# First mixer's head sums in column tiles, and factors spread through device memory

## What is computed

```python
def _rms_norm(x, w):
    xf = x.astype(jnp.float32)
    y = xf * lax.rsqrt(jnp.mean(xf * xf, axis=-1, keepdims=True) + EPS)
    return (y * w.astype(jnp.float32)).astype(x.dtype)
def _rms_f32(xf):
    return xf * lax.rsqrt(jnp.mean(xf * xf, axis=-1, keepdims=True) + EPS)
def _l2norm(xf):
    return xf * lax.rsqrt(jnp.sum(xf * xf, axis=-1, keepdims=True) + EPS)
...
    q = _l2norm(q.reshape(bsz, s, h, d)) * (d ** -0.5)
    k = _l2norm(k.reshape(bsz, s, h, d))
...
    o = _rms_f32(_from_chunks(o))
```

## Time and profile before

| | |
|---|---|
| median of 3 runs | 1778.69 us (1778.51 to 1781.49) |
| profiled execution | 1779.13 us |
| its span, first to last instruction | 1777.3 us |
| mean granted TensorE clock | 0.998 |
| PE busy | 1752.7 us, 99% |
| DVE busy | 1152.7 us, 65% |
| ACT busy | 722.4 us, 41% |
| DMA queue of SP | 172.01 MB, 30.0% of 16 engines |

### The profile page before, as it was taken

One profiled execution on the slowest core, in us unless ns is written; L12 is line 12 of the kernel. 1 busy time (PEld: TensorE's weight loads), 2 busy tenths in 40 slices (PEclk: granted clock), 3 DMA queues, 4 the chain that ended last, 5 costly groups with the idle time before them and its releaser, 6 DMA issues.

```text
span 1777.3 us, 22802 instructions
## 1 busy us (share of the span) xinstructions
PE 1752.7 (99%) x9216; PEld 1393.8 (78%) x9216; DVE 1152.7 (65%) x1685; ACT 722.4 (41%) x1026; POOL 0.2 (0%) x4
## 2 busy tenths in 40 slices
PE   8999989999999999999999999999998999999999
PEld 6777867888888887776888888888764888888887
DVE  5876944777776344777777777433997667777521
ACT  4257424544444333445644444323224544444321
POOL 0000000000000000000000000000000000000000
PEclk9999999999999999999999999999999999999999
DMA  6222111322332322311332222232652222332222
GB/s 232 95 95 72 43 33 42 134 95 95 98 102 79 110 97 94 107 44 52 123 103 95 95 95 94 96 98 96 191 173 82 96 95 95 98 102 95 88 97 79
DMA packets 57969, 173.60 MB, mean 98 GB/s; under 512 B 8316, under 2 KB 9084, under 8 KB 57736
## 3 DMA queue, kind: packets, MB, share of 16 engines
q1 hardware_dynamic: 57720, 172.01, 30.0%
q10 hardware_dynamic: 144, 0.13, 0.0%
HBM read 161.32 MB, written 2.12 MB: 92 GB/s over the span
## 4 chain that ended last, share of the span: by engine, by line
PE 96%; DVE 2%; ACT 1%; issue 1%; DMA 0%; SPq 0%; DVEq 0%; ACTq 0%
PE bank L201 95%; DVE mixer_arena L1216 1%; PE bank L645 0%; DMA res<-in_x 0%; DVE mixer_arena L1224 0%; DVE res L1216 0%; DVE even_arena L1752 0%; ACT even_arena L777 0%; DVE mixer_arena L1515 0%; ACT wh L777 0%; DVE mixer_arena L1220 0%; DVE wl L1216 0%; DVE gdn_low_ygl L1216 0%; PE bank L413 0%; ACT conf_rstd L777 0%
## 5 line engine op out<-in xcount | busy, mean ns | idle before, releaser
L201 PE MATMUL bank<-nh,wh 128*128 128x512 f32 x1504 | 596.0, 396 | 0.0
L777 ACT ACTIVATE wh<-raw 128x1024 fp32r<-128x1024 f32 (+2 forms) x308 | 306.8, 998 | 697.3 <-PE bank L201 688.6
L201 PE MATMUL bank<-nh,wl 128*128 128x512 f32 x1504 | 586.6, 390 | 0.9 <-issue 0.9
L201 PE MATMUL bank<-nl,wh 128*128 128x512 f32 x1504 | 586.2, 390 | 0.0
L1216 DVE TENSOR_TENSOR wl<-raw,wh 128x1024 fp32r<-128x1024 f32 (+2 forms) x308 | 352.8, 1146 | 242.1 <-ACT wh L777 241.3
L201 PEld LDWEIGHTS bank<-nh,wh 128*128 128x128 f32 x1504 | 282.7, 188 | 69.5 <-issue 11.4
L201 PEld LDWEIGHTS bank<-nl,wh 128*128 128x128 f32 x1504 | 282.9, 188 | 61.7 <-issue 3.4
L201 PEld LDWEIGHTS bank<-nh,wl 128*128 128x128 f32 x1504 | 282.7, 188 | 60.5 <-issue 1.4
L201 PE MATMUL bank<-ff_yh,wh 128*128 128x512 f32 x528 | 205.4, 389 | 0.0
L201 PE MATMUL bank<-ff_yl,wh 128*128 128x512 f32 x528 | 205.4, 389 | 0.0
L201 PE MATMUL bank<-ff_yh,wl 128*128 128x512 f32 x528 | 205.4, 389 | 0.0
(11 more groups left out here) (188 smaller groups left out, 1420.6 us busy)
## 6 DMA issues: line engine op xcount, KB each, us to landing
raw<-in_ff_a_up SPq DMA_DIRECT2D x44, 512.0 KB, 3.4
raw<-in_ff_b_up SPq DMA_DIRECT2D x44, 512.0 KB, 3.4
raw<-in_ff_c_up SPq DMA_DIRECT2D x44, 512.0 KB, 3.4
raw<-in_w_in SPq DMA_DIRECT2D x32, 512.0 KB, 3.6
raw<-in_pw SPq DMA_DIRECT2D x24, 512.0 KB, 3.7
raw<-in_even_in SPq DMA_DIRECT2D x16, 512.0 KB, 3.5
conf_shifted<-conf_pad SPq DMA_DIRECT2D x112, 66.0 KB, 2.0
raw<-in_ff_a_down_a SPq DMA_DIRECT2D x8, 512.0 KB, 3.5
```

What stands on the lines that cost most here:

```text
L201: return e.matmul(out, lhsT, rhs, start=start, stop=stop, skip_group_check=True)
L777: return e.activation(out, in_, func, **kw).then_inc(n.give(sem), 1)
```

## The change

Head sums: the twelve sums of full width become three groups of four. In a group g each sum has 32 columns of ones as its stationary operand and writes 32 rows of one bank, so that the four heads' sums stand in rows 0, 32, 64 and 96 of that bank. One logarithm and one exponential then serve four heads. As the factor is no longer on every partition, SP stores the four rows to device memory (store_heads) and reads them back as one row of 2048 values into all 128 partitions (spread_heads), over the four squares' slots; DVE waits for that transfer (head_spread) before the first of each four scales. ACT takes the first root before it squares the queries. The squares of the retention outputs move to other slots.

Value factor: root_columns and ACT's copy are gone. SP stores row 0 of c.r and issues four transfers of 128 values, one value to a partition, at pieces 9 and 11 of the first mixer and at pieces even+9 and even+10 of the even mixer.

```diff
--- before.py
+++ after.py
@@ -349,12 +341,12 @@
         mm(bank[4 + h % 2][:, j * P:S], m1.rv[:, j, h * P:(h + 1) * P], m1.pt[:, s % 3, 0:S - j * P],
            j == 0, j == TB - 1).then_inc(n.give(c.ret_done), 1)
 
-    def head_sum(i):
-
-        e.wait_ge(c.head_squared, i + 1)
-        if i >= 6:
-            e.wait_ge(c.head_logged, i - 5)
-        mm(bank[m1.sum_bank[i % 6]][:, :], c.ones[:, :], m1.hsq[i], True, True).then_inc(n.give(c.head_summed), 1)
+    def head_sums(g):
+
+        e.wait_ge(c.head_squared, HEADS * (g + 1))
+        for h in range(HEADS):
+            done = mm(bank[m1.sum_bank[g]][h * Q:(h + 1) * Q, :], c.ones[:, 0:Q], m1.hsq[HEADS * g + h], True, True)
+        done.then_inc(n.give(c.head_summed), 1)
 
     for i in range(12):
         j = i % 2 if i else 6
...
@@ -378,15 +370,12 @@
             done.then_inc(n.give(c.gcols_done), 1)
         if i == 9:
             e.wait_ge(c.gcols_ready, 1)
-            for q in range(4):
-                head_sum(q)
+            head_sums(0)
         if i == 10:
             e.wait_ge(c.ret_copied, HEADS)
-            for q in range(4, 6):
-                head_sum(q)
+            head_sums(1)
         if i == 11:
-            for q in range(6, 12):
-                head_sum(q)
+            head_sums(2)
 
 
     hs = [slice(h * P, (h + 1) * P) for h in range(HEADS)]
...
@@ -596,11 +585,8 @@
             vacate(6)
             e.wait_ge(c.accb_done, DK - 1)
             mm(bank[6][:, :], c.ones[:, :], m2.accb, True, True).then_inc(n.give(c.stat_done), 1)
-        else:
-            e.wait_ge(c.second_sum, 2)
-            root_columns(7)
-
-    token_pieces(c.nl_ready, 2 * DK, {0: (0,), 1: (1,), 3: (3,)}, second_sum)
+
+    token_pieces(c.nl_ready, 2 * DK, {0: (0,), 1: (1,)}, second_sum)
     e.wait_ge(c.gate_scaled, 2)
     mm(bank[4][0:AH, :], m2.gate_sums, m2.ln, True, True).then_inc(n.give(c.gate_summed), 1)
     take(5)
...
@@ -608,7 +594,7 @@
     take(6)
     piece(6, c.nh, c.nl, range(DK))
     e.wait_ge(c.even_ready, 16 * 5)
-    small["read"] = (c.rcol_ready, 2)
+    small["read"] = (c.root_done, 3)
     att_sum(0)
     take(0)
     piece(0, c.nh, c.nl, range(DK))
...
@@ -888,9 +866,6 @@
         if s == 2:
             e.wait_ge(c.cols_rest, 16)
             act(m1.ea[0:HEADS, :], col(c, "a_log", parts=HEADS), ACT.Exp, c.ea_ready)
-        if s == 3:
-            e.wait_ge(c.rcol_done, 1)
-            act(c.rcol[:, :], bank[6][:, 0:TB], ACT.Copy, c.rcol_ready)
     for w in range(RING):
         feed()
     e.wait_ge(c.gates_for_act, 1)
...
@@ -909,10 +884,11 @@
         for q in range(4):
             act(m1.hsq[first + q], src[:, q, :], ACT.Square, c.head_squared)
 
-    def roots_of(first, count, scale):
-        e.wait_ge(c.head_summed, first + count)
-        head_root(lambda q: bank[m1.sum_bank[(first + q) % 6]][:, :], lambda q: m1.hsq[first + q], c.head_logged, c.head_root,
-                  count, scale)
+    def roots_of(g, scale):
+        e.wait_ge(c.head_summed, g + 1)
+        act(m1.hroot[g], bank[m1.sum_bank[g]][:, :], ACT.Ln, c.head_logged, bias=c.eps[:, 0:1], scale=scale)
+        settle()
+        act(m1.hroot[g], m1.hroot[g], ACT.Exp, c.head_root, scale=-0.5)
 
     for i in range(12):
         feed()
...
@@ -954,13 +930,12 @@
             e.wait_ge(c.ret_copied, HEADS)
             square_heads(m1.oret, 4)
         if i == 10:
+            roots_of(0, 1.0)
             square_heads(m1.gq, 8)
-            roots_of(0, 4, 1.0)
         if i == 11:
-            roots_of(4, 2, 1.0 / P)
-
-    roots_of(6, 2, 1.0 / P)
-    roots_of(8, 4, 1.0)
+            roots_of(1, 1.0 / P)
+
+    roots_of(2, 1.0)
     feed()
     for q in (9, 10, 11):
         silu(q)
...
@@ -1372,7 +1345,7 @@
     for w in range(RING):
         arrive()
         if w == RING - 1:
-            e.wait_ge(c.rcol_ready, 1)
+            e.wait_ge(c.rcol_ready, 16 * TB)
             for t in range(TB):
                 ts(m1.rv[:, t, :], bank[t][:, :], c.rcol[:, t:t + 1], ALU.mult, c.evac)
         feed()
...
@@ -1415,7 +1388,8 @@
         tt(chunk_of_heads(m1.qk, h), m1.d, m1.below.unsqueeze(1).to_broadcast([P, TB, P]), ALU.min, c.dec_ready)
 
     def head_scale(i):
-        e.wait_ge(c.head_root, i + 1)
+        if i % HEADS == 0:
+            e.wait_ge(c.head_spread[i // HEADS], 16)
         x = (m1.gk, m1.oret, m1.gq)[i // 4][:, i % 4, :]
         if i // 4 == 2:
             stt(x, x, float(P) ** -0.5, m1.hsq[i], ALU.mult, ALU.mult, c.head_scaled)
...
@@ -1933,6 +1907,16 @@
             e.wait_ge(c.lo_ready, s - RAWS + 1)
         load(c.raw[:, s % RAWS, 0:w], d[name][i], c.raw_ready[s % RAWS])
 
+    def store_heads(g):
+
+        e.wait_ge(c.head_root, g + 1)
+        load(d["head_rows"][g:g + 1, :].rearrange("o (h s) -> (o h) s", s=S), m1.hroot[g][0:P:Q, :], c.rows_stored)
+
+    def spread_heads(g):
+
+        e.wait_ge(c.rows_stored, 16 * (g + 2))
+        load(m1.hfactor[g], d["head_rows"][g:g + 1, :].broadcast_to([P, HEADS * S]), c.head_spread[g])
+
     def spread(h):
 
         load(m1.qd[:, h, :], d["decay_rows"][h:h + 1, :].broadcast_to([P, S]), c.spread_ready)
...
@@ -1971,6 +1955,13 @@
     load(c.cols[:, DK:], d["cols"][:, DK:], c.cols_rest)
     even = PIECE_AT[("even_in", 0)]
     for s in range(3, NPIECES):
+        if s in (9, even + 9):
+            e.wait_ge(c.root_done, 1) if s == 9 else e.wait_ge(c.second_sum, 2)
+            load(d["root_row"], c.r[0:1, :], c.root_stored)
+        if s in (11, even + 10):
+            e.wait_ge(c.root_stored, 16 if s == 11 else 32)
+            for t in range(TB):
+                load(c.rcol[:, t:t + 1], d["root_row"][:, t * P:(t + 1) * P].rearrange("o p -> p o"), c.rcol_ready)
         if s == 4:
             load(m1.tables, d["tables"], c.mix_ready)
             load(m1.gate_sums, d["ab_sums"], c.mix_ready)
...
@@ -1992,6 +1983,10 @@
             e.wait_ge(c.gdn_low, TB)
             load(m2.gate_w, d["f"], c.even_ready)
             load(m2.gate_sums, d["f_sums"], c.even_ready)
+        if 29 <= s < 32:
+            store_heads(s - 29)
+        if s == 31:
+            spread_heads(2)
         if s == 31:
             e.wait_ge(c.head_scaled, 12)
             load(m1.levels, d["levels"], c.mask_ready)
...
@@ -2013,9 +2008,11 @@
             for h in range(HEADS):
                 spread(h)
         if s == even + 11:
-            e.wait_ge(c.rows_stored, 32)
+            e.wait_ge(c.rows_stored, 16 * 5)
             for h in range(4):
                 forget_row(h)
+        if 29 <= s < 31:
+            spread_heads(s - 29)
     for k in range(DK):
         e.wait_ge(c.evac, GROUPS - DK + k + 1)
         e.dma_start(out[:, k, :], c.res[:, k, :]).then_inc(c.out_stored, 16)
...
@@ -2025,7 +2022,8 @@
 def build(nc, d, out):
     with ExitStack() as ctx:
         c = allocate(nc, ctx)
-        d = dict(d, decay_rows=nc.dram_tensor("decay_rows", (HEADS, S), F32).ap(),
+        d = dict(d, root_row=nc.dram_tensor("root_row", (1, S), F32).ap(),
+                 head_rows=nc.dram_tensor("head_rows", (3, HEADS * S), F32).ap(), decay_rows=nc.dram_tensor("decay_rows", (HEADS, S), F32).ap(),
                  forget_rows=nc.dram_tensor("forget_rows", (AH, S), F32).ap())
 
         def arena(stack, phase, base, **spec):
...
@@ -2059,7 +2057,8 @@
             tables=A[:, 43 * S:45 * S], cos=slots(A, 43), sin=slots(A, 44), z=slots(A, 45), az=slots(A, 46), ln=slots(A, 47),
             gate_w=A[:, 48 * S:48 * S + DK * Q], gate_sums=A[:, 49 * S:49 * S + 2 * Q],
             rows=slots(A, 22), d=c.sq[:, 0, :].rearrange("p (t s) -> p t s", s=P),
-            hsq=[slots(A, i) for i in (19, 20, 21, 22, 16, 17, 4, 5, 12, 13, 14, 15)], sum_bank=(6, 7, 2, 3, 4, 5),
+            hsq=[slots(A, i) for i in (19, 20, 21, 22, 4, 5, 6, 7, 12, 13, 14, 15)], hfactor=[A[:, i * S:(i + HEADS) * S] for i in (19, 4, 12)],
+            sum_bank=(6, 7, 2), hroot=[c.sq[:, 0, :], c.sq[:, 1, :], c.acc[:, :]],
             oret=slots(A, 0, 4), kbg=slots(A, 4, 4), kd=slots(A, 8, 4), vb=slots(A, 12, 4), gg=slots(A, 0, 4),
             levels=A[:, 16 * S:16 * S + LEVELS * Q // 2], Z3=A[:, 16 * S + P:16 * S + P + S // 2], T3=slots(A, 17), U3=slots(A, 22),
             Z5=slots(A, 27), Z6=A[0:2 * Q, 25 * S:27 * S], T6=A[0:2 * Q, 23 * S:25 * S], U=slots(A, 31, 4),
```

More of the change, by code:

```diff
@@ L162, in allocate @@
         bank=[ctx.enter_context(nc.psum_tensor(f"bank{i}", [P, S], F32)) for i in range(8)],
+        head_spread=[ctx.enter_context(nc.semaphore(f"head_spread{i}")) for i in range(3)],
         raw_ready=[ctx.enter_context(nc.semaphore(f"raw_ready{i}")) for i in range(RAWS)],
@@ L285, in token_sums @@
         mm(bank[j][:, :], c.ones[:, :], c.acc[:, :], True, True).then_inc(n.give(c.stat_done), 1)
-    def root_columns(j):
-        for t in range(TB):
-            done = mm(bank[j][:, t:t + 1], c.r[0:8, t * P:(t + 1) * P], c.ident[0:8, 0:1], True, True)
-        done.then_inc(n.give(c.rcol_done), 1)
     def feed_forward(i):
@@ L827, in residual @@
```

(10 more changed lines are left out.)

7 lines of the change are left out of this document (2 added, 5 removed).

## The result

| | before | changed |
|---|---|---|
| median of 5 runs each | 1778.69 us (1777.94 to 1781.49) | 1786.88 us (1783.83 to 1788.16) |
| ratio to before | | 1.0034, 95% interval 1.0022 to 1.0046 |
| profiled execution | 1779.13 us | 1783.83 us |
| its span | 1777.3 us | 1782.1 us |
| mean granted TensorE clock | 0.998 | 0.993 |

The change makes the kernel slower, by 0.34%. So the sign is that of the forecast; how much is lost differs from one set of executions to the next, and the experiments show what it hangs on.

The account below looks back on a forecast made before the run. The prediction took PE, 99% busy, as the bound, with DVE's head scales ending almost together with it before the first chunk. Terms +2.3 +1.7 -1.2 +0.5 = +3.3 gave 1782.4 profiled, 1782.0 us as median; range 1775.5 to 1787.

Parts of the forecast that it names:

- Two chains that end together: Before the first chunk transpose, PE and DVE finish within a quarter of a microsecond; shortening one alone gains nothing.
- step 1: Before the second quartet PE waits 2.5 us for ACT's squares of the retention outputs, losing 2.5 of 7.8 us spared.
- step 4: The 1 MB spread of factors into all partitions takes 5.7 us, bounds 5.2 and 7.7.
- steps 5 and 6: Before the first chunk, third store waits for second spread; third spread lands last; PE waits about 7.8 us, cost +2.3.
- The clock behind the wait: After the long wait before the first chunk, PE runs at 1.2 GHz for most of 4 us: +1.7, bounds 0 to 2.
- First mixer's columns: Four 8-row matmuls for the value factor go, their replacement transfers hidden by prefetch: -1.2 us, bounds -1.2 to 0.
- Even mixer: Value columns by transfers make DVE wait 1.0 us and delay the first key sum: +0.5, bounds -0.4 to +2.
- as early as before: Rival before the first chunk: cheaper spreads or an unheld third store, -0.3 there, total -0.1, 1778.6 us; chance 0.22.
- dear spreads: Rival before the first chunk: spreads cost 7.0 us or more each, +4.9 there, total 1784.6 us or more; chance 0.24.

Follow-up runs that it names:

- once more: The changed kernel run again without edits, a second comparison against the kernel before: 1783.06 us, ratio 1.0020.
- heads only: The changed kernel with the value factor's columns made as before, on PE and ACT: 1787.37 us, 1.0042 of the kernel before the change.
- fillers: The changed kernel with 24 products that nothing reads in PE's long wait before the first chunk: 1781.88 us, 1.0010 of the kernel before.
- stores first: The changed kernel with the third store issued ahead of the second spread in SP's queue: 1784.22 us, 1.0028 of the kernel before.
- columns only: The kernel before with only the value columns made by transfers, in both mixers: 1780.61 us, 0.9999 of the kernel before.
- Queries second: The changed kernel with the queries' quartet second and the retention's third, its scales behind PE's wait: 1780.73 us, 1.0005 of the kernel before.
- queries at full width: Queries' sums at full width before the retention's quartet, keys and retention still by quartets and spreads: 1778.02 us, 0.9988 of the kernel before.

## Why the prediction was right in sign, and where it was wrong

- **Two chains that end together**: right, and the heart of it. PE is spared 7.8 us of its own sums (11.0 to 3.2 busy, as reckoned) and gets none of it.
- **The second quartet's wait** (step 1): 2.5 forecast, 2.30 measured.
- **The price of a spread** (step 4), 5.7 each: wrong as one number. Over all traces it is 6.7 to 8.5 with a weight load issued 1.1 to 1.9 us ahead, and 4.3 to 4.7 with none nearer than 3 us. The 4.4 us estimated from the Trainium skill's figures beside the prediction ("DMA: Bandwidth & Descriptors", "Anatomy of one DMA") fits a spread that is alone in the queue (4.7 in the first profile); for the other two (7.6 and 7.2) the measurement differs and decides.
- **What ends the long wait** (steps 5 and 6): right in three traces of four, by way of two wrong prices. The store is held up behind the second spread (6.0 us forecast, 6.8 measured three times, 4.6 once) and the third spread comes last in "once more", "heads only" and "fillers". The second spread costs 1.3 to 2.8 us more than the 5.7 that I took and the third 1.0 to 1.3 less, so that their sum (11.5 to 12.9) is near the forecast's 11.4; that the errors largely cancel is luck. In the changed kernel's first profile the third spread lands just as DVE comes to it, and the second spread with eight scales behind it sets the start; "stores first" does the same. Forecast 7.8 us of wait and +2.3 relative to block 9; measured 5.8 and +0.85 in the first profile, 7.0 and +3.5 in the second (1.5 of it from the clock).
- **The clock behind the wait**: right in kind, 1.7 forecast, 2.2 measured at the chunk (4.8 less 2.6). The sum gave one wait a fall and the other none: the second quartet's wait of 2.3 us, which step 1 forecast, takes the clock down as well in some executions ("once more": 163 to 167 us, "heads only": 165 to 169), and the third quartet then comes 1.5 and 1.6 us later. Over the executions 9 to 14 us are lost where before loses 6, and fillers in the long wait bring that back. This is the term that was too small: +1.7 in the sum, where the mean loss rises by 3.3 us in the second comparison and by about 8 in the first. The other thing the sum took for granted is the profile it was made against: the execution of before shown there has a clock of 0.998, the mean over 79 is 0.9966 and the median time of those is 1780.75.
- **First mixer's columns**, -1.2: block 9 ended 1.83 us earlier, 0.4 of it from the first load, and 1.25 in "columns only"; held.
- **Even mixer**, +0.5: measured +0.2, from 33.16 to 33.39 us between gate products and key sum, with DVE waiting 0.5 for the columns where I had 1.0. Right in kind, a little smaller. Both column edits together are nothing, as "columns only" shows.
- The **rivals**: the chunk's start, +0.85 and +3.5, lies above the -0.3 of "as early as before", on either side of the forecast's +2.3 and below the +4.9 of "dear spreads". The last has the better total for the first comparison (1784.6 and more against 1786.88), and two of three spreads did cost its 7 us, but the first spread held up nothing, and it had the loss in the wait where the runs show it in the clock.

**What stays open.** The eleven profiles (before, changed and the nine runs) show 19 falls in the solve, and each begins during an idle stretch of PE of 1.06 to 2.03 us or at most 1.8 us behind it: a wait of 1.45 us for DVE that every kernel has (1.07 us for DVE in one case), or a stop without a releaser ("issue") whose place and length differ from trace to trace. Why one such stretch is followed by a fall and the next is not ("once more" has two and no fall), why a fall lasts 3.5 or 7 us, and where the stops come from was not settled; kernels with and without the long wait have them. "Queries second" loses 10.5 us without a wait over 2.3 us at the chunk, and why it loses 3 more than "queries at full width" is open. And where the unprofiled runs of the changed kernel lose their clock is inferred from the means and from what the fillers do, not seen.

## What to carry to other kernels

Before freeing an engine, look for who else finishes at the same moment: a second chain that ends within a quarter of a microsecond turns the whole gain into a wait. A wait put into PE's stream costs its length and then, in many of the executions here, the half clock behind it; so it pays to take work out of what PE waits for (the retention's scales), to send through memory only what has slack (keys and retention, not the queries), and to fill the last one or two microseconds with products that nobody reads. And give a transfer the price it has in its place in the queue, behind what is issued just ahead of it, not an average.

## What was unexpected of the hardware

- A wait of 2.3 us was enough to take the granted clock to 0.5 in some executions (the quartet at 162.77 took 1.93 us) and not in others (161.12, 1.06 us); that one of 1.8 us does so now and then is inferred from the means alone.
- Shorter stops went before a fall as well: in the solve 2.0 us (fall from 244.9 in the changed kernel), 1.45 us (fall from 258.6) and 1.06 us (fall from 239.2 before the change). During such a fall PE is busy throughout (8.00 us of 8 from 244 to 252, granted 0.57), and it comes up to 1.8 us behind the stop, so a window over the fall alone hides what went before it.
- Six idle-time products, 1.5 us of work in a kernel of 1775, were worth 0.18% by the two ratios (0.9970 against 0.9988, each against before; the intervals overlap slightly).
- A store of 8 KB took 4.6 us from issue to being seen behind a broadcast of 1 MB in one trace and 6.4 to 6.8 in four, at most 1.7 to 2.7 otherwise.
- The 1 MB broadcast of one 8 KB row into 128 partitions took 4.3 to 4.7 us alone and 6.7 to 8.5 with a half-megabyte load issued 1 to 2 us ahead.
